# Two-layer macaron decoder step, float32 split into high and low parts: the RMSNorm factors of the tokens by ones products, ln/exp and a Newton step in place of columns, pow and diagonals

## The reference, cut to what matters

```
def rmsnorm(x, g):
    y = x * lax.rsqrt(jnp.mean(x * x, axis=-1, keepdims=True) + EPS)      # EPS = 1e-6
    return y * g

def mixer(h, ...):                                                        # both halves of D_MIX = 1024
    xl, yl, q, k, v, g, gd = jnp.split(h @ p['w_in'], IN_SPLITS, axis=-1)
    xc, new_conv = causal_conv(xl, ...)
    hl, h_last = rg_lru(xc, ...)
    lru_out = rmsnorm(hl * jax.nn.gelu(yl), p['lru_norm'])                # over D_LRU = 512
    o, S_fin = gla_chunked(q, k, v, ...)                                  # 4 heads
    o = rmsnorm(o, p['gla_norm'])                                         # over 128, head by head
    return jnp.concatenate([lru_out, o * silu(g)]) @ p['w_out']

def layer(x, ...):
    x = x + 0.5 * rmsnorm(swiglu(rmsnorm(x, pre[0]), ffn 0), post[0])
    x = x + rmsnorm(mixer(rmsnorm(x, pre[1])), post[1])
    x = x + 0.5 * rmsnorm(swiglu(rmsnorm(x, pre[2]), ffn 1), post[2])
```

## Time and profile before

| | |
|---|---|
| median of 3 runs | 2229.8 us (2228.38 to 2230.82) |
| the profiled execution, its own time | 2230.11 us |
| its span, first to last instruction | 2228.3 us |
| mean granted TensorE clock | 0.997 |
| TensorE matmuls busy | 2207.4 us (99%) |
| VectorE, ScalarE, GpSimd busy | 1360.4, 1177.6, 753.6 us (61, 53, 34%) |

### The profile page before, as it was taken

One profiled execution on the slowest core, in us unless ns is written; L12 is line 12 of the kernel. 1 busy time (PEld: TensorE's weight loads), 2 busy tenths in 40 slices (PEclk: granted clock), 3 DMA queues, 4 the chain that ended last, 5 costly groups with the idle time before them and its releaser, 6 DMA issues.

```text
span 2228.3 us, 40420 instructions
## 1 busy us (share of the span) xinstructions
PE 2207.4 (99%) x16870; PEld 2183.1 (98%) x16870; DVE 1360.4 (61%) x1771; ACT 1177.6 (53%) x1832; POOL 753.6 (34%) x802
## 2 busy tenths in 40 slices
PE   8999999999999999999999999999999999999998
PEld 8999999999999999999999999999999999999998
DVE  6555757657785557745574557576578756475454
ACT  6534547536675445543454355574467654464443
POOL 4012512516545225521251124134264533252112
PEclk9999999999999999999999999999999999999999
DMA  6555555445544455555555555554454444655553
GB/s 225 167 161 163 167 167 157 143 122 164 160 143 138 130 175 157 166 165 163 163 165 164 162 164 161 167 161 133 127 178 151 143 133 131 182 162 159 163 165 129
DMA packets 102405, 350.62 MB, mean 157 GB/s; under 512 B 11440, under 2 KB 16560, under 8 KB 102224
## 3 DMA queue, kind: packets, MB, share of 16 engines
q1 hardware_dynamic: 100992, 346.76, 51.3%
q10 hardware_dynamic: 1232, 1.27, 0.2%
HBM read 343.12 MB, written 4.87 MB: 156 GB/s over the span
## 4 chain that ended last, share of the span: by engine, by line
PE 93%; DVE 3%; POOL 2%; issue 2%; ACT 0%; DMA 0%; SPq 0%; DVEq 0%; POOLq 0%
PE psD L447 87%; DVE wl L1051 1%; POOL ssum L1470 1%; PE psS L453 1%; PE psM L589 1%; DVE hl L1103 1%; PE psM L565 1%; DVE y L1089 0%; DVE x L1093 0%; PE psM L671 0%; PE psM L642 0%; PE psM L648 0%; DMA x<-in_xT 0%; PE psM L595 0%; PE psS L491 0%
## 5 line engine op out<-in xcount | busy, mean ns | idle before, releaser
L447 PE MATMUL psD<-hh,wh 128*128 128x288 f32 x3712 | 1109.4, 299 | 4.9 <-DVE hl L1103 3.1
L447 PE MATMUL psD<-hl,wh 128*128 128x288 f32 x3712 | 1096.7, 295 | 0.0
L447 PE MATMUL psD<-hh,wl 128*128 128x288 f32 x3712 | 1093.5, 295 | 0.0
L1051 DVE TENSOR_TENSOR wl<-raw,wh 128x1024 fp32r<-128x1024 f32 (+1 forms) x656 | 818.7, 1249 | 133.4 <-ACT wh L759 133.3
L759 ACT ACTIVATE wh<-raw 128x1024 fp32r<-128x1024 f32 (+1 forms) x656 | 672.5, 1027 | 104.8 <-DMA raw<-in_w_gu 52.5
L447 PEld LDWEIGHTS psD<-hh,wh 128*128 128x128 f32 x3712 | 697.6, 188 | 11.4 <-issue 6.1
L447 PEld LDWEIGHTS psD<-hh,wl 128*128 128x128 f32 x3712 | 700.6, 189 | 0.0
L447 PEld LDWEIGHTS psD<-hl,wh 128*128 128x128 f32 x3712 | 698.9, 188 | 0.9
L1707 POOL TENSOR_TENSOR hidl<-hid,hidh 128x288 fp32r<-128x288 f32 x176 | 210.1, 1194 | 930.7 <-ACT hidh L1001 930.7
L447 PE MATMUL psD<-hidh,wh 128*128 128x288 f32 x1408 | 417.5, 296 | 0.0
L447 PE MATMUL psD<-hidl,wh 128*128 128x288 f32 x1408 | 415.5, 295 | 0.0
(11 more groups left out here) (192 smaller groups left out, 1460.4 us busy)
## 6 DMA issues: line engine op xcount, KB each, us to landing
raw<-in_w_gu SPq DMA_DIRECT2D x352, 512.0 KB, 3.6
raw<-in_w_d SPq DMA_DIRECT2D x128, 448.0 KB, 3.2
raw<-in_w_in SPq DMA_DIRECT2D x80, 512.0 KB, 3.6
raw<-in_w_d SPq DMA_DIRECT2D x64, 512.0 KB, 3.6
raw<-in_w_out SPq DMA_DIRECT2D x32, 512.0 KB, 3.6
gates<-in_w_ax SPq DMA_DIRECT2D x4, 512.0 KB, 4.5
S<-in_st_gla SPq DMA_DIRECT2D x4, 512.0 KB, 4.6
out_gla_s<-S SPq DMA_DIRECT2D x4, 512.0 KB, 5.6
```

What stands on the lines that cost most here:

```text
L447: mm = e.matmul(out, w[:, kt * P:(kt + 1) * P], t[:, kt, :], start=(kt == 0 and part == 0), stop=(kt == KT - 1 and part == 2))
L1051: e.tensor_tensor(wl[u % RING][:, 0:width], raw[u % RING][:, 0:width], wh[u % RING][:, 0:width].bitcast(F32), ALU.subtract).then_inc(lo_re ...
```

## The change

The pow, the columns, the diagonals and their spreads are gone. A token's sum is formed on all 128 partitions at once, by a product of a 128x128 matrix of ones with the sum of squares, so that it needs no spreading. The factor (mean + eps)^(-1/2) comes as exp(-0.5 ln(mean + eps)) on ScalarE (`first_guess`), and VectorE betters it by one Newton step, three operations of 288 elements (`newton`).

- Split sums: in all boundaries but the quick ones, also in the one beside the second group's input projection, ScalarE makes the high part of `ssum` (`split_sums`, slots `start` and `end`), VectorE the low part (`low_sums`, same slots), TensorE the two fp32r products two slots later, ScalarE ln and exp (asked for at its slot `start` + 1), VectorE the Newton step at `start` + 2.
- Quick sums: one float32 ones product on the unsplit `ssum`; in the last boundaries two, one for `ssum` and one for the last square.
- A floor in place of the columns' one: `floor` [128x288], added by VectorE (`add_floor`) ahead of ln.
- Mixer: ScalarE squares the outputs as it takes them from PSUM (two more operations per chunk), splits 5 tiles at once (slot 30), VectorE makes the low parts (slot 31), TensorE runs ten products at slot 32, ScalarE ln and exp at slots 32 and 33, VectorE three Newton steps at slots 34, 35 and 36; the values begin one slot later (T_VALUES = 37). The LRU squares are summed at slot 29 in place of 15.
- The scaling of y and the values read the factor from SBUF in place of PSUM. Of the 22 matmuls that keep TensorE busy ahead of the very end 12 are left.

```diff
-TAIL_WARM = [256] * 12, [256] * 10
+TAIL_WARM = [256] * 12
...
-T_LRU_SUM = 15
-T_VALUES = T_SUMS + 5
+T_LRU_SUM = 29
+T_VALUES = T_SUMS + 6
...
 # tensor
+        def token_sums(g, quick=False, final=False):
             sums_free()
+            out = psS[:, 0, 0:T]
             if final:
...
+                e.matmul(out, ones[:, :].bitcast(F32), ssum[g][:, :], start=True, stop=False)
                 e.wait_ge(sq_ready[g], DT * (group_event[g] + 1))
+                e.matmul(out, ones[:, :].bitcast(F32), sq[g][(DT - 1) % 2][:, :], start=False, stop=True).then_inc(sums_done, 1)
+            elif quick:
+                e.wait_ge(sq_used[g], (DT - 1) * (group_event[g] + 1))
+                e.matmul(out, ones[:, :].bitcast(F32), ssum[g][:, :], start=True, stop=True).then_inc(sums_done, 1)
             else:
+                splits[0] += 1
+                e.wait_ge(ssl_ready, splits[0])
+                e.matmul(out, ones[:, :], ssh[g][:, :], start=True, stop=False)
+                e.matmul(out, ones[:, :], ssl[g][:, :], start=False, stop=True).then_inc(sums_done, 1)
...
+            later = 0 if quick else 2
             for slot in range(end + 3):
+                if slot == start + later:
...
+                    token_sums(g, quick, final)
...
+                if slot == end + later:
+                    token_sums(g, quick)
                 yield
...
 # tensor, attention
+                if slot == T_SUMS + 1:
                     sums_free()
+                    e.wait_ge(stl_ready, i + 1)
+                    e.wait_ge(s_ready, 3 * i + 3)
+                    for k in range(STATS):
+                        out = psM[:, k - 1, 0:T] if k else psS[:, 0, 0:T]
+                        e.matmul(out, ones[:, :], sth5[g][:, k, :], start=True, stop=False)
+                        mm = e.matmul(out, ones[:, :], stl5[g][:, k, :], start=False, stop=True)
+                    mm.then_inc(sums_done, 1)
...
 # scalar
+        def split_sums(g):
+            e.wait_ge(sq_used[g], (DT - 1) * (group_event[g] + 1))
+            e.activation(ssh[g][:, :], ssum[g][:, :], ACT.Copy).then_inc(ssh_ready, 1)
+
+        def first_guess(g, floored=False, keep=False):
...
+            e.preload_act_table_set("natural_log_exp_and_others")
+            if floored:
+                e.wait_ge(stat_read, event[0])
+                ln = steps.mark(e.activation(guess[:, :], factor[:, :], ACT.Ln))
             else:
+                e.wait_ge(sums_done, event[0])
+                ln = steps.mark(e.activation(guess[:, :], psS[:, 0, 0:T], ACT.Ln, scale=1.0 / D, bias=epsc[:, :]))
+            if keep:
+                e.activation(floor[g][:, :], psS[:, 0, 0:T], ACT.Identity, scale=EPS / D, bias=eps2c[:, :])
+            steps.after(ln)
+            e.activation(guess[:, :], guess[:, :], ACT.Exp, scale=-0.5).then_inc(guess_ready, 1)
...
+            for slot in range(end + 2):
+                if slot in (start, end) and not quick:
+                    split_sums(g)
+                if slot == (start if quick else start + 1):
+                    first_guess(g, floored=st != 1)
...
+                if slot == (end if quick else end + 1):
+                    first_guess(g, keep=st != 0)
...
 # vector
+        def newton(out, floored=False):
...
+            e.wait_ge(guess_ready, factors[0])
+            if floored:
+                steps.mark(e.tensor_tensor(factor[:, :], factor[:, :], guess[:, :], ALU.mult))
+                steps.after()
+            else:
+                e.scalar_tensor_tensor(factor[:, :], psS[:, 0, 0:T], D * EPS, guess[:, :], ALU.add, ALU.mult).then_inc(stat_read, 1)
+                e.wait_ge(stat_read, event[0])
+            steps.mark(e.scalar_tensor_tensor(factor[:, :], factor[:, :], -0.5 if floored else -0.5 / D, guess[:, :], ALU.mult, ALU.mult))
+            steps.after()
+            e.scalar_tensor_tensor(out[:, :], factor[:, :], 1.5, guess[:, :], ALU.add, ALU.mult).then_inc(factor_ready, 1)
...
         def rescale(g, m, n):
             tiles = y[g][:, m:m + n, :]
...
-            e.tensor_tensor(tiles, tiles, psS[:, 0, 0:T].unsqueeze(1).broadcast_to([P, n, T]), ALU.mult).then_inc(y_normed[g], 1)
+            e.tensor_tensor(tiles, tiles, factor[:, :].unsqueeze(1).broadcast_to([P, n, T]), ALU.mult).then_inc(y_normed[g], 1)
...
+                if slot in (start, end) and not quick:
+                    low_sums(g)
+                if slot == start + hop - 1 and st != 1:
+                    add_floor(g)
                 if slot == start + hop:
+                    newton(factor, floored=st != 1)
...
 # gpsimd: root() and its calls removed
```

More of the change, by code:

```diff
@@ L449, in unit @@
             mm.then_inc(unit_done, 1)
-        def columns(src, first, stop, k=0, at=0):
-            for t in range(NTC):
-                mm = e.matmul(psS[0:TC, 0, 288 + at + t:289 + at + t], src[:, t * TC:(t + 1) * TC], means[:, k:k + 1],
-                              start=(first and t == 0), stop=stop, skip_group_check=True)
-            return mm
         def sums_free():
-            if last_use:
-                e.wait_ge(*last_use[-1])
-        def token_sums(g, normed=None, final=False):
+            if event[0]:
+                e.wait_ge(stat_read, event[0])
@@ L1039, in _ @@
         event = [0]
-        kept = [0]
-        spreads = [0]
-        spread_of = []
+        factors = [0]
+        splits = [0]
         lows = [0]
@@ L1520, in boundary @@
             for slot in range(end + 1):
-                if slot == start:
-                    root(NTC, floor=g if st != 1 else None, quick=quick)
                 k = (slot - start - hop - 1) * at_once
@@ L1538, in boundary @@
                         add_square(g, t)
-                if slot == end:
-                    root(NTC, keep=g if st != 0 else None, quick=quick)
                 yield
```

303 lines of the change are left out of this document (107 added, 196 removed).

## The result

The changed kernel takes 2234.2 us in the median of 19 runs (2233.7 to 2238.1), the kernel before, beside it on the same chip, 2231.7 (2227.6 to 2233.4). The ratio is 1.0015, 95% interval 1.0009 to 1.0022: slower by 2.5 us by the medians and by 3.4 by the ratio, within the 0.2% that counts as no change, where 10 us less were forecast. Its profiled execution has a span of 2232.2 us, 3.9 more than before, at a mean granted clock of 0.993 (before 0.997).

The account below looks back on a forecast made before the run. TensorE's matmul stream plus the few places where it waits was taken as the bound. Savings less charges summed to -10.0 us against the profiled 2230.1: 2220.1, or 2219.8 as median; range 2204 to 2228.

Parts of the forecast that it names:

- Start: At the kernel's start the first gate waits for the factor, which was to come sooner: 1.4 us saved.
- the first place: Start of the quick boundary beside `wout`: first scaling later by 0.75 us in each layer (0 to 2), 1.5 lost.
- the last boundary of group 0: Two float32 products replace twice the columns there: 0.6 us saved.
- the tail: Behind the last sums at the kernel's end, a longer chain to the scalings: 1.1 us lost (0.5 to 2).
- the mixers: Four mixers: 10.5 us saved on the stream, 3.2 given back waiting for low tiles at slot 32, net 7.3.
- the second place: First sums beside the second input projection: ScalarE's later work delays the stream 2.8 us per layer, 5.6 in all.
- Fifteen split sums at 0.53: Ordinary boundaries: removing each block of columns saves 0.53 us of TensorE's stream, 8.0 us for fifteen sums.
- the loads: ScalarE's table loads around ln and exp: 1.28 us each, with no added drain charged.
- Contention 0 to 0.6: Beside `wout`, the second scaling reads two SBUF operands beside GpSimd's additions: 0 to 0.6 us more.
- the slower rival: Second input projection: the late tap delays tiles 1 to 3 and the clock falls, 2242 us; chance 0.08.
- Signs: Expected in the trace: waits for `stl`, low operand and gates, 48 more table loads; wrong if tile 1's gates don't wait.
- The doubled waits: Rival: waits throughout come to twice those taken, +10.9 us, 2230.7; chance 0.12.

Follow-up runs that it names:

- the two pairs of profiles: Kernel before and changed kernel, each profiled twice unedited; the changed kernel's span ended 3.9 us later in the first pair, 2.3 in the second.
- experiment 5: Changed kernel with the mixer's last Newton operation writing its factors to PSUM, where the values read them: 2233.1 us, 1.0010 to the kernel before.
- experiment 7: Changed kernel with quick, unsplit float32 sums in the boundary beside the second group's input projection: 2230.2 us, 0.9996 to the kernel before.
- Experiment 3: Changed kernel with the factor for the scalings of y written to and read from PSUM: 2226.1 us, 0.9981 to the kernel before.
- experiment 2: Changed kernel with ScalarE's ln and exp one slot later, behind tile 1's tap, beside the second input projection: 2233.4 us, 1.0016 to the kernel before.
- the twelve edited versions: Nine single edits of the changed kernel and three combinations of them, measured from 2218.8 to 2235.9 us.
- experiments 1: Changed kernel with the mixer's last Newton step and its values one slot earlier: 2235.3 us, 1.002 to the kernel before.

## Why the prediction was wrong

- *Start.* 1.4 less forecast, 1.6 measured. Right.
Of the 12 to 14 us between the forecast and the two pairs of profiles 9 to 10 lie at the first place, 1.8 at the last boundary of group 0, 1.1 in the tail and 2.4 in the mixers; the second place came out some 3 better.

- *Fifteen split sums at 0.53.* The start of the unit behind moves by 0.45, the next ones by 0.08. Right. So were the float32 product (0.58 for 0.55) and the loads: at 590.61 a load ends where the sigmoid starts, 591.90, as in the earlier trace rows.
- *Mixers, 7.3.* The wait of the products was sized well, 0.98 for 0.8. Left out were the waits that VectorE's new backlog brings in the slots behind: 0.4 for a low hidden tile, four times, and 0.6 for a low value, twice. Each mixer gave 1.2 to 1.3 in place of 1.8.
- *First place, "I take 0.75 in each layer".* This is the step that failed. With the 0.76 that the quick sum was to save there the forecast had the place at nothing; it lost 4.4 to 6.0 us per layer. The reason given, that the stream's savings there are worth nothing, was right and taken too narrowly. It began at the first scaling, 543.13. Work that no saving in the stream shortens begins with the values at slot 37: values, low parts on GpSimd, squares' sum, factor, scaling, additions, operands. TensorE came to `wout` 6.1 us sooner and to the second unit of `win` only 1.1 (565.5, before 566.6). And the values, which the forecast moved by a slot and charged nothing, had nearly doubled beside GpSimd (0.50 to 0.86 and 0.92; experiment 5). VectorE's stretch from the first scaling to the last operand, taken as full, also got a gap: 1.73 us ahead of 542.19.
- *"Contention 0 to 0.6".* The bound was set for one scaling, without a row of an operation with two SBUF inputs beside GpSimd. Such rows stand in the trace of before: two low operands take 2.03 in the earlier trace rows, while one at 599.61 in experiment 7, with GpSimd idle, takes 0.50. Each place where `factor` is read was one to price: the values, the second `win`, the last boundary of group 0 (the sum there saved its 0.6 and a little more, but 1.9 was lost at unit 594), the tail (1.1 forecast, 2.2 measured). Experiment 3 gives 8 us for the scalings alone, by moving the factor, with the wait that its new place needs, and nothing else.
- *Second place, 2.8 per layer.* Up to tile 2 this came as forecast, and by the chain that the forecast gave: the sigmoids end at 592.79 (593.05 forecast), `ig` at 593.87 (594.1), `xc` at 595.69 (594.9, or 596.4 beside GpSimd's additions), and VectorE takes unit 8 at 603.12 (603.3). Counted from unit 166, unit 176 starts 2.7 to 3.1 us later than before. Two things were missing. ScalarE's chain is not alone: VectorE's Newton step, scaling and lengthened taps end within 0.4 us of it (experiments 2 and 7). And 1.5 us come back at tile 3. Before, a stretch at half speed follows that tile's wait in every profile; in the changed kernel none does. In three of four cases one lies behind tile 2 instead and tile 3's wait shrinks from 2.15 to 0.6, in the fourth there is none and the wait is 2.14. With the 0.5 that the sum at slot 18 saves, the place costs 0.7. The price of 2.8 was right for the sums and wrong for the place.
- *The clock.* It stood only in the slower rival, at other places and at 1.7 us each; by the products' starts it is 1.5. New waits of 2 us bring half speed behind them: four such stretches in each profile of after (the first has a fifth near its start), at most 1.5 us each, two in each of before.
- *Signs.* The waits for `stl` (0.81, four times), for the last low operand (2.05) and of the gates of tiles 1 and 2 (1.26 and 1.98) came as said, and ScalarE's table loads rose from 68 to 116. The forecast also named what would prove it wrong: a stream that waits in the ffn stages. It does, 1.67 us at unit 594 and 0.4 four times for a low hidden tile.
- *Rivals.* None came in its form. The doubled waits were nearest in time (2230.7), by other waits.

Open: whether the stretches behind the small products become more frequent with the change (the twelve edited versions have them at 31 of 48 places, before at 3 of 8), and how much of the loss at the first place is the values' length and how much their later slot, since experiments 1 and 5 move each alone and the first unit of the second `win` takes most of either gain back.

## What to carry to other kernels

When an operand moves from PSUM to SBUF and the other one lies there already, look at each reader of the moved tile that starts while GpSimd works: here such a scaling took 2.58 us in place of 1.35, while those with GpSimd idle kept their length. Before crediting a saving in TensorE's stream, follow each chain that the stream will next wait for back to its first link, since what is saved between that link and the wait is worth nothing. A new wait in the stream can also cost the clock behind it, up to 1.5 us here for a wait of 2. And where two chains end at the same time, moving one alone shows nothing (experiment 2).

## What was not expected of the hardware

- The same VectorE value takes 0.50 us from PSUM and 0.86 to 0.92 from SBUF on average beside GpSimd's subtractions. A scaling that starts inside a GpSimd addition ends 1.21 to 1.22 us behind it (four tiles) or 0.61 (two tiles), whatever its start.
- At `wout` a wait of 2.1 us ahead of a stream that is busy otherwise is followed in 17 of 18 cases by up to 3.4 us at 1.2 GHz; with 2.30 us of unused products in it, by none. Behind waits of 2.0 to 2.15 in the second `win` it came in some cases and not in others.
- Such a stretch also follows the mixer's small products without any longer wait, in some executions and not in others of the same kernel.
